# Attention transposes released by the exponentials, and a rotation split over four units

## The chip, the cores and the metric

The kernel runs on one core of one Trainium2 chip. Its five engines take their instructions in order and meet through semaphores: TensorE (PE in the profile; PEld is its weight load) multiplies and transposes into PSUM banks, VectorE (DVE) and ScalarE (ACT) do arithmetic on PSUM and SBUF, GpSimd (POOL) and SyncE (SP) mostly start DMAs. The metric is the device time of one execution in microseconds.

## The reference, cut to what matters

The whole program is a two-layer mixer block, then a gated delta-net block, a sliding-window attention and an eight-expert feed-forward. The change touches three attentions. In each of the two layers there are a differential attention (A), the forgetting attention (B, the "second" one) and a retention (C); the window attention is the "local" one.

```
def _forgetting_attention(q, k, v, log_f):      # B, 4 heads of 128, 256 tokens
    F = jnp.cumsum(log_f, axis=1)
    s = einsum(q, k) * scale + F_q - F_k
    p = softmax(where(causal, s, -inf))
    return p @ v

def _rotary(t, pos):                            # on q and k of the retention C
    t1, t2 = t[..., :half], t[..., half:]
    return concat([t1 * cos - t2 * sin, t1 * sin + t2 * cos])

def swa_sink_attention(...):                    # W, 16 heads of 64, window 128, a sink logit
    p = softmax(concat([s + bias, sink]))[..., :-1]
    return (p @ v) @ w_out
```

B and W keep the softmax's numerator as it comes from the exponential and divide the head's output by the row sum. So what is transposed is the exponential itself, and the reciprocal of the row sum enters only when the output leaves PSUM. A is different: there two maps are scaled by their reciprocals and combined before the transpose.

## The kernel before, in words

Every fp32 weight chunk of 1 MB (a half chunk, 128 x 2048) goes through a fixed path: a DMA into one of four slots `W`, ScalarE's `high(1)` (line 1670, two instructions) rounds it into one of two slots `W_high`, VectorE's `low(1)` (line 2167, two instructions) writes the remainder to `W_low`, and TensorE multiplies it in three products (lines 844 to 846), 24 matmuls for a half chunk. `high` of half chunk n waits until TensorE has done half chunk n-2. This projection work is called the background (`next(bg)`).

The order of every engine is written out by hand. The second attention of a layer is a loop over eight units u = 8 to 15 (four heads, two query tiles; an even u has one key tile, 128 scores a row, an odd u two, 256). In unit u each engine does:

- TensorE: the scores of unit u+1, one half chunk of the background, `attend_T` (line 1056: the transposes of unit u's exponentials, line 1064), `attend_out` of unit u-1 (line 1077). After the last unit come the output of unit 15, the transposes of the rotated q and k ("cT", which wait for `zC_ready`), of A's normed output ("yA", which wait for `y_ready`), and then the next half chunk of the background. That one needs two PSUM banks, of which the second is free only when VectorE has read out the output of unit 15.
- ScalarE: `exps(u+1)` (line 1778), `evict_probsT` of unit u (line 1655, the transposed exponentials to SBUF), `high(1)`; after the `high` of unit 12 also `root(8)` (line 1792), a square root for A's norm, for which the activation table is switched there and back.
- VectorE: `mask_b(u+1)` (lines 2503 and 2505: scores from PSUM plus mask, and the row maximum), the reciprocal of unit u's row sum (line 2764, which signals `probs`), in odd units the bias addition of a finished background chunk (line 2157, two), `b_out(u-1)` (line 2636), `low(1)`, and then extra work: in units 9 and 10 `rotate(t)`, twelve operations for one token tile (lines 2745 to 2755), in unit 12 `sums_a` (sums of squares of A's output), in unit 13 `scale_a` (its norm, which signals `y_ready`). After unit 15 follows `b_out(15)`.

So VectorE's reciprocal of unit u stands behind mask u+1, which stands behind all extra work of unit u-1, and TensorE's `attend_T` of unit u waits for that reciprocal through `probs`. The exponential of unit u, signalled by `exped`, is made one unit earlier.

The window attention has 16 units of the same form with three score buffers; there `window_T(u-1)` comes behind the scores of unit u+1, and VectorE's reciprocal is line 3294. Its projections are woven between the units.

## Time and profile before

| | |
|---|---|
| three runs | 2946.49, 2950.98, 2953.47 us; median 2950.98 |
| the profiled execution | 2955.86 us, of which the span is 2954.0 |
| PE / DVE / ACT busy | 2668.4 / 2180.4 / 1516.2 us (90 / 74 / 51% of the span) |
| mean granted TensorE clock | 0.944 of 2.4 GHz |
| the chain that ended last | PE 63%, DVE 22%, ACT 7%, issue 4%, DMA 3% |
| DMA share by fortieths of the span | 1 to 5 tenths in most of the two layers, 9 in the experts |
| second attention and what follows it, layer 0 | transposes of unit 9 at 238.9 us, next half chunk after the attention at 302.6 |
| the same in layer 1 | 880.3 us and 942.8 |
| window attention | 1808 to 1876 us |

The span is cut by stage, and each stage has its own limit: an average such as TensorE's 90% does not tell whether a given wait of 3 us costs 3 us. A timeline row gives the start, the duration, the engine and the line, and in brackets how long the engine had been idle before and which instruction released it.

### The profile page before, as it was taken

The numbers are of one execution on the slowest core, as the hardware profiler recorded it, in microseconds if no ns is written. First come the engines' busy times: TensorE is split into PE (matmuls) and PEld (weight loads), VectorE is DVE, ScalarE is ACT, GpSimd is POOL, SyncE is SP. The second block draws the span as 40 slices with busy tenths as digits, with TensorE's granted clock in tenths as the row PEclk, the third lists the DMA queues.
The fourth block names the chain that finished last, engine by engine and source line by source line (L and its number), as shares of the span: only waits on it lengthen the run. The fifth ranks groups of instructions, "written<-read, shape, count | busy, mean of one in ns | idle before, by whom it ended". The sixth has DMA issues, their size and how long they took to land.

```text
span 2954.0 us, 36711 instructions
## 1 busy us (share of the span) xinstructions
PE 2668.4 (90%) x14052; PEld 2275.1 (77%) x14052; DVE 2180.4 (74%) x2746; ACT 1516.2 (51%) x1782; POOL 24.2 (1%) x46
## 2 busy tenths in 40 slices
PE   7988888898987889987889987789999999999997
PEld 6766678876776679877788966678888888888885
DVE  6766487778666677755577546678989889898886
ACT  2233434434334345435324334457777777777774
POOL 0000000000000000000000000000000000000000
PEclk9889999999899899988999998789999999999998
DMA  9633345576533355442105582369999998999984
GB/s 357 254 129 131 120 157 213 199 284 247 203 132 128 111 189 207 158 157 101 68 16 183 184 242 100 125 248 368 346 351 367 346 369 344 351 365 347 373 341 184
DMA packets 104753, 671.67 MB, mean 227 GB/s; under 512 B 11984, under 2 KB 12240, under 8 KB 27136
## 3 DMA queue, kind: packets, MB, share of 16 engines
q1 hardware_dynamic: 97584, 622.08, 56.8%
q0 software_dynamic: 6992, 47.19, 4.8%
q8 instruction: 116, 1.90, 0.3%
q14 instruction: 61, 0.50, 0.0%
HBM read 665.03 MB, written 4.19 MB: 227 GB/s over the span
## 4 chain that ended last, share of the span: by engine, by line
PE 63%; DVE 22%; ACT 7%; issue 4%; DMA 3%; PEld 2%; DVEq 0%; SPq 0%; ACTq 0%; PEldq 0%
PE bank L844 18%; PE bank L845 18%; PE bank L846 18%; DVE W_low L2167 8%; ACT W_high L1670 3%; PE bank L1252 3%; DVE work L2252 1%; PE bank L1550 1%; DMA arena<-in_w_layer 1%; DMA W<-in_w_layer 1%; DVE arena L2157 1%; DMA W<-in_w_middle 1%; DVE work L2484 1%; PEld bank L844 1%; DMA R<-in_rows_middle 1%
## 5 line engine op out<-in xcount | busy, mean ns | idle before, releaser
L2167 DVE TENSOR_TENSOR W_low<-W,W_high 128x1024 fp32r<-128x1024 f32 x426 | 496.7, 1207 | 352.6 <-ACT W_high L1670 348.8
L1670 ACT ACTIVATE W_high<-W 128x1024 fp32r<-128x1024 f32 x426 | 422.3, 1040 | 456.0 <-PE bank L846 211.8
L845 PE MATMUL bank<-W_low,arena_parts 128*128 128x512 f32 x1112 | 438.5, 394 | 0.0
L844 PE MATMUL bank<-W_high,arena_parts 128*128 128x512 f32 x968 | 390.8, 404 | 16.0 <-DVE W_low L2167 10.9
L846 PE MATMUL bank<-W_high,arena_parts 128*128 128x512 f32 x968 | 382.7, 395 | 0.0
L846 PE MATMUL bank<-hT_high,W_low 128*128 128x256 f32 x1184 | 340.6, 288 | 0.0
L844 PE MATMUL bank<-hT_high,W_high 128*128 128x256 f32 x1072 | 311.4, 291 | 20.1 <-DVE W_low L2167 12.0
L844 PE MATMUL bank<-W_high,hT_high 128*128 128x512 f32 (+3 forms) x688 | 285.8, 415 | 29.5 <-DVE W_low L2167 10.1
L845 PE MATMUL bank<-hT_low,W_high 128*128 128x256 f32 x1072 | 306.6, 286 | 0.0
L845 PE MATMUL bank<-W_low,hT_high 128*128 128x512 f32 (+4 forms) x736 | 294.0, 399 | 0.0
L846 PE MATMUL bank<-W_high,hT_low 128*128 128x512 f32 (+3 forms) x688 | 274.6, 399 | 0.0
L844 PE MATMUL bank<-arena_parts 128*128 128x512 f32 x672 | 269.3, 401 | 1.5 <-issue 1.5
L846 PE MATMUL bank<-arena_parts 128*128 128x512 f32 x672 | 263.2, 392 | 0.0
L845 PEld LDWEIGHTS bank<-W_low,arena_parts 128*128 128x128 f32 x1112 | 212.3, 191 | 42.9
L846 PEld LDWEIGHTS bank<-hT_high,W_low 128*128 128x128 f32 x1184 | 233.6, 197 | 0.0
L844 PEld LDWEIGHTS bank<-W_high,arena_parts 128*128 128x128 f32 x968 | 185.0, 191 | 60.1 <-DVE W_low L2167 15.0
L844 PEld LDWEIGHTS bank<-hT_high,W_high 128*128 128x128 f32 x1072 | 208.8, 195 | 27.2 <-DVE W_low L2167 17.5
L846 PEld LDWEIGHTS bank<-W_high,arena_parts 128*128 128x128 f32 x968 | 184.5, 191 | 41.0
L845 PEld LDWEIGHTS bank<-hT_low,W_high 128*128 128x128 f32 x1072 | 209.1, 195 | 0.1
L844 PEld LDWEIGHTS bank<-W_high,hT_high 128*128 128x128 f32 x688 | 145.1, 211 | 63.5 <-DVE W_low L2167 22.5
L845 PE MATMUL bank<-arena_parts 128*128 128x512 f32 x456 | 178.2, 391 | 0.0
L845 PEld LDWEIGHTS bank<-W_low,hT_high 128*128 128x128 f32 x736 | 157.1, 213 | 25.5
(418 smaller groups left out, 4884.8 us busy)
## 6 DMA issues: line engine op xcount, KB each, us to landing
W<-in_w_layer SPq DMA_DIRECT2D x170, 1024.0 KB, 4.9
W<-in_w_expert SPq DMA_DIRECT2D x148, 1024.0 KB, 4.8
arena<-in_w_expert SPq DMA_DIRECT2D x114, 1024.0 KB, 5.0
W<-in_w_middle SPq DMA_DIRECT2D x58, 1024.0 KB, 5.0
arena<-in_w_layer POOLq DMA_DIRECT2D x40, 1024.0 KB, 6.4
consts<-in_w_expert SPq DMA_DIRECT2D x37, 1024.0 KB, 4.9
R<-in_w_expert SPq DMA_DIRECT2D x37, 1024.0 KB, 5.0
R<-in_rows_layer SPq DMA_DIRECT2D x70, 256.0 KB, 5.7
```

Of the source, the lines that this page charges most:

```text
L844: mm(bank, lhs[0], rhs[0], start=start, stop=False)
L845: mm(bank, lhs[0], rhs[1], start=False, stop=False)
L846: return mm(bank, lhs[1], rhs[0], start=False, stop=stop)
L1252: last = mm(bank[:, i * P:(i + 1) * P], lhs(i), rhs(i), start=True, stop=True)
L1550: last = turn_over(bank[:, i * P:(i + 1) * P], hid_tok[:, c % 2, i * P:(i + 1) * P], ident)
L1670: do(high_slot(at, w)[:, cols], raw(at, w)[:, cols], ACT.Copy).then_inc(main_highs.filled[main_highs.slot(at, w)], 1)
L2157: tt(dst, bank[:, 0:width], r[:, 0:width], ALU.add).then_inc(*psum.frees(v.at, job))
L2167: tt(lows(at, w)[:, cols], raw(at, w)[:, cols], high_slot(at, w)[:, cols].bitcast(F32), ALU.subtract).then_inc(*low_ready.event(at))
L2252: i = stt(acc, part, csil[:, f:f + 1], acc, ALU.mult, ALU.add)
L2484: stt(c[:, 2:S], u[:, 0:S - 2], taps[:, j:j + 1], c[:, 2:S], ALU.mult, ALU.add).then_inc(*hid_pre.event(v.at))
```

## The change

Two things change. The transposes of the second and of the window attention (not of A) wait for the exponential's signal `exped`, and the rotation is cut in halves: `rotate(t, s)` does six operations, and units 9, 10, 11 and 12 have one half each where units 9 and 10 had two. `zC_ready` is signalled behind units 10 and 12. To make room, `sums_a` moves from unit 12 to 13, `scale_a` from 13 to 14, and ScalarE's `root(8)` from behind unit 12's `high` to behind unit 13's. The number of instructions stays the same on every engine.

```diff
--- before.py
+++ after.py
@@ -1055,7 +1055,7 @@
 
             def attend_T(kind, h_, t, u, maps, src=None):
                 hand_back()
-                pe.wait_ge(*probs.nth(at, u + 1))
+                pe.wait_ge(*(probs if kind == "A" else exped).nth(at, u + 1))
                 pe.wait_ge(*psum.vacant(at, (kind + "t", h_, t)))
                 bank = banks[psum.slot(at, (kind + "t", h_, t))]
                 for m in range(maps):
@@ -1882,7 +1882,7 @@
                         exps(u + 1, (u + 1) % NT, 1)
                     evict_probsT("B", (u - 8) // NT, u % NT, u, 1)
                     high(1)
-                    if u == 12:
+                    if u == 13:
                         root(8)
                 tiles("cT", 2, cT, qkT_ready)
                 high_tiles("yA", 1, yATs)
@@ -2735,25 +2735,24 @@
 
 
 
-                def rotate(t):
-                    for s in range(2):
-                        z = zCqk[:, t, s * 512:(s + 1) * 512].rearrange("p (h f) -> p h f", h=C_HEADS)
-                        t1, t2 = z[:, :, 0:64], z[:, :, 64:128]
-                        w = [work[:, i * 256:(i + 1) * 256].rearrange("p (h f) -> p h f", h=C_HEADS) for i in range(3)]
-                        cs = cos[:, t, :].unsqueeze(1).to_broadcast([P, C_HEADS, 64])
-                        sn = sin[:, t, :].unsqueeze(1).to_broadcast([P, C_HEADS, 64])
-                        tt(w[0], t1, cs, ALU.mult).then_inc(dve_done, 1)
-                        dve.wait_ge(dve_done, v.count())
...
-                        tt(t2, w[0], w[2], ALU.add).then_inc(dve_done, 1)
-                        dve.wait_ge(dve_done, v.count())
+                def rotate(t, s):
+                    z = zCqk[:, t, s * 512:(s + 1) * 512].rearrange("p (h f) -> p h f", h=C_HEADS)
+                    t1, t2 = z[:, :, 0:64], z[:, :, 64:128]
+                    w = [work[:, i * 256:(i + 1) * 256].rearrange("p (h f) -> p h f", h=C_HEADS) for i in range(3)]
+                    cs = cos[:, t, :].unsqueeze(1).to_broadcast([P, C_HEADS, 64])
+                    sn = sin[:, t, :].unsqueeze(1).to_broadcast([P, C_HEADS, 64])
+                    tt(w[0], t1, cs, ALU.mult).then_inc(dve_done, 1)
+                    dve.wait_ge(dve_done, v.count())
...
+                    tt(t2, w[0], w[2], ALU.add).then_inc(dve_done, 1)
+                    dve.wait_ge(dve_done, v.count())
 
                 mask_b(8)
                 for u in range(8, 16):
@@ -2768,12 +2767,13 @@
                     if u > 8:
                         b_out(u - 1)
                     low(1)
-                    if u == 12:
+                    if u == 13:
                         sums_a()
-                    if u == 13:
+                    if u == 14:
                         scale_a()
-                    if u in (9, 10):
-                        rotate(u - 9)
+                    if 9 <= u < 13:
+                        rotate((u - 9) // 2, (u - 9) % 2)
+                    if u in (10, 12):
                         dve.nop().then_inc(*zC_ready.event(v.at))
                 b_out(15)
                 dve.nop().then_inc(*y_ready.event(v.at))
```

On TensorE no instruction moves; only what the first transpose of a unit waits for. The piece below is from the difference of TensorE's instructions with their waits, at unit 9 of layer 0 (`scores` holds the exponentials, `bank_freed` and `product_done` are PSUM hand-overs).

```order
 L846 MATMUL bank<-W_high,hT_low 128x512
-L1064 MATMUL bank<-consts,scores 128x128 [waits product_done1,bank_freed4,probs]
+L1064 MATMUL bank<-consts,scores 128x128 [waits product_done1,bank_freed4,exped]
 L1064 MATMUL bank<-consts,scores 128x128
 L1077 MATMUL bank<-arena,probsT 128x128 [waits bank_freed5,probsT_ready]
```

The signal named at the end of the wait list is the reciprocal's before and the exponential's now; the product and the bank that it also waits for stay.

On VectorE the rotation moves. First as it was, from the end of unit 9's first half rotation on into unit 10, layer 0 (`W_low` is the background's `low`, `small` the row sums):

```order
L2751 TENSOR_TENSOR arena<-work 128x4x64 [waits dve_done]
L2753 TENSOR_TENSOR work<-arena,consts 128x256 [waits dve_done]
L2755 TENSOR_TENSOR arena<-work 128x4x64 [waits dve_done]
L2503 SCALAR_TENSOR_TENSOR scores<-bank,consts 128x256 [waits dve_done,product_done6]
L2505 TENSOR_REDUCE small<-scores 128x1 [waits bank_freed6]
L2764 RECIPROCAL small<-small 128x1 [waits exped,masked]
L2636 TENSOR_SCALAR arena<-bank,small 128x128 [waits product_done2,probs]
```

These are the last three of twelve rotation operations, and the mask of unit 11 and the reciprocal of unit 10 stand behind all twelve. Then the changed kernel at the same place, from the end of unit 9's `low` on:

```order
L2744 TENSOR_TENSOR work<-arena,consts 128x256
L2746 TENSOR_TENSOR work<-arena,consts 128x256 [waits dve_done]
L2748 TENSOR_TENSOR work<-arena,consts 128x256 [waits dve_done]
L2750 TENSOR_TENSOR arena<-work 128x4x64 [waits dve_done]
L2752 TENSOR_TENSOR work<-arena,consts 128x256 [waits dve_done]
L2754 TENSOR_TENSOR arena<-work 128x4x64 [waits dve_done]
L2503 SCALAR_TENSOR_TENSOR scores<-bank,consts 128x256 [waits product_done6,dve_done]
L2505 TENSOR_REDUCE small<-scores 128x1 [waits bank_freed6]
L2763 RECIPROCAL small<-small 128x1 [waits exped,masked]
```

Six operations stand ahead of the mask now; the other six come behind unit 10's `low`, and the same again in units 11 and 12.

On ScalarE the square root with its two table loads moves back by one unit. The piece is from the difference of ScalarE's instructions, layer 0, units 13 and 14 (`probsT` are the transposed exponentials, `W_high` is the background's `high`):

```order
 L1670 ACTIVATE W_high<-W 128x1024 x2
+L1778 ACTIVATE scores,small<-scores,small 128x128
+L1655 ACTIVATE probsT<-bank 128x256
+L1670 ACTIVATE W_high<-W 128x1024 x2
 L1792 ACT_TABLE_LOAD
 L1792 ACTIVATE small<-small 128x8
 L1778 ACT_TABLE_LOAD
-L1778 ACTIVATE scores,small<-scores,small 128x128
-L1655 ACTIVATE probsT<-bank 128x256
-L1670 ACTIVATE W_high<-W 128x1024 x2
 L1778 ACTIVATE scores,small<-scores,small 128x256
```

The exponentials that stand behind the table loads are now those of unit 15, not of unit 14.

## Rows read from the trace of the kernel before

**Rows 1.** What TensorE's transposes (line 1064) waited for: releaser, us in total, times.
```profile
  DVE small L2764: 20.5, 8
  DVE small L3294: 8.3, 5
```
**Rows 2.** Timeline of TensorE, layer 0: transposes of units 9, 10, 11, 13, 14; next half chunk.
```profile
238.94 0.41 PE L1064 MATMUL bank<-consts,scores 128*128 128x128 f32 x2 [0.30 <-PE bank L846]
...
250.49 0.33 PE L1064 MATMUL bank<-consts,scores 128*128 128x128 f32 x1 [3.27 <-DVE small L2764]
...
261.29 0.44 PE L1064 MATMUL bank<-consts,scores 128*128 128x128 f32 x2 [3.88 <-DVE small L2764]
...
279.30 0.44 PE L1064 MATMUL bank<-consts,scores 128*128 128x128 f32 x2 [1.34 <-DVE small L2764]
...
289.46 0.44 PE L1064 MATMUL bank<-consts,scores 128*128 128x128 f32 x1 [1.89 <-DVE small L2764]
...
302.57 0.47 PE L844 MATMUL bank<-W_high,hT_high 128*128 128x512 f32 x1 [0.65 <-DVE arena L2636]
```
**Rows 3.** Timeline of VectorE, layer 0, from unit 9's rotation to unit 10's.
```profile
243.73 0.42 DVE L2745 TENSOR_TENSOR work<-arena,consts 128x256 f32<-128x256 f32 x1
...
248.79 0.42 DVE L2755 TENSOR_TENSOR arena<-work 128x256 f32<-128x256 f32 x1
249.36 0.42 DVE L2503 SCALAR_TENSOR_TENSOR scores<-bank,consts 128x256 f32<-128x256 f32 x1
...
252.53 2.36 DVE L2167 TENSOR_TENSOR W_low<-W,W_high 128x1024 fp32r<-128x1024 f32 x2 [0.79 <-ACT W_high L1670]
254.81 0.42 DVE L2745 TENSOR_TENSOR work<-arena,consts 128x256 f32<-128x256 f32 x1
```
**Rows 4.** Timeline of ScalarE in the same unit: exponentials of unit 11, then `high`.
```profile
250.27 0.51 ACT L1778 ACTIVATE scores<-scores,small 128x256 f32<-128x256 f32 x1 [7.98 <-DVE small L2505]
...
251.37 2.01 ACT L1670 ACTIVATE W_high<-W 128x1024 fp32r<-128x1024 f32 x2 [0.17 <-ACT probsT L1655]
```
**Rows 5.** Timeline of VectorE, layer 0: sums, mask 14, bias additions, norm, mask 15, last output.
```profile
275.34 0.69 DVE L2716 TENSOR_TENSOR work<-arena 128x512 f32<-128x512 f32 x1
...
278.43 0.29 DVE L2503 SCALAR_TENSOR_TENSOR scores<-bank,consts 128x128 f32<-128x128 f32 x1
...
279.28 1.42 DVE L2157 TENSOR_TENSOR h<-bank,R 128x512 f32<-128x512 f32 x2
...
284.95 0.20 DVE L2336 RECIPROCAL small<-small 128x8 f32<-128x8 f32 x1
...
288.33 0.43 DVE L2503 SCALAR_TENSOR_TENSOR scores<-bank,consts 128x256 f32<-128x256 f32 x1 [0.15 <-DVE arena L2732]
...
302.08 0.34 DVE L2636 TENSOR_SCALAR arena<-bank,small 128x128 f32<-128x128 f32 x1
```
**Rows 6.** Timeline of ScalarE: the table load back to the exponential, layer 0.
```profile
279.12 1.28 ACT L1778 ACT_TABLE_LOAD   x1 [0.48 <-DVE small L2505]
```
**Rows 7.** Stretches: us, busy of PE, PEld, DVE, ACT, POOL, granted clock, DMA share, GB/s.
```profile
261.30:265.30 4.00, 4.00 (x15) 3.32 (x15) 3.47 (x5) 2.66 (x5) 0.00 (x0) 0.62 0.25 98
302.60:316.20 13.60, 13.30 (x58) 10.53 (x58) 4.37 (x6) 9.59 (x9) 0.00 (x0) 1.00 0.27 87
```
**Rows 8.** A stretch of layer 1, behind the transposes of unit 11; same columns.
```profile
902.30:907.00 4.70, 4.69 (x13) 3.94 (x14) 3.92 (x5) 2.67 (x5) 0.00 (x0) 0.50 0.23 91
```
**Rows 9.** Timeline of layer 1: VectorE's rotation in unit 9, TensorE's half chunk after the attention.
```profile
884.76 0.42 DVE L2745 TENSOR_TENSOR work<-arena,consts 128x256 f32<-128x256 f32 x1
...
942.78 0.47 PE L844 MATMUL bank<-W_high,hT_high 128*128 128x512 f32 x1 [0.66 <-DVE arena L2636]
```
**Rows 10.** Timeline of the window attention: last step of exponential 0, transposes 0 and 4.
```profile
1808.65 0.19 ACT L2050 ACTIVATION_READ_ACCUMULATOR arena<-arena,small 128x1 f32 x1
...
1810.01 0.69 PE L1064 MATMUL bank<-consts,arena 128*128 128x128 f32 x2 [5.16 <-DVE small L3294]
...
1825.57 0.44 PE L1064 MATMUL bank<-consts,arena 128*128 128x128 f32 x2 [0.77 <-DVE small L3294]
```

More of the change, by code:

```diff
@@ L2734, in scale_a @@
                     dve.nop().then_inc(*rows.frees(v.at, ("gdiff", 0)))
-                def rotate(t):
-                    for s in range(2):
-                        z = zCqk[:, t, s * 512:(s + 1) * 512].rearrange("p (h f) -> p h f", h=C_HEADS)
-                        t1, t2 = z[:, :, 0:64], z[:, :, 64:128]
-                        w = [work[:, i * 256:(i + 1) * 256].rearrange("p (h f) -> p h f", h=C_HEADS) for i in range(3)]
-                        cs = cos[:, t, :].unsqueeze(1).to_broadcast([P, C_HEADS, 64])
-                        sn = sin[:, t, :].unsqueeze(1).to_broadcast([P, C_HEADS, 64])
-                        tt(w[0], t1, cs, ALU.mult).then_inc(dve_done, 1)
-                        dve.wait_ge(dve_done, v.count())
-                        tt(w[1], t2, sn, ALU.mult).then_inc(dve_done, 1)
-                        dve.wait_ge(dve_done, v.count())
-                        tt(w[2], t1, sn, ALU.mult).then_inc(dve_done, 1)
-                        dve.wait_ge(dve_done, v.count())
-                        tt(t1, w[0], w[1], ALU.subtract).then_inc(dve_done, 1)
-                        dve.wait_ge(dve_done, v.count())
-                        tt(w[0], t2, cs, ALU.mult).then_inc(dve_done, 1)
-                        dve.wait_ge(dve_done, v.count())
-                        tt(t2, w[0], w[2], ALU.add).then_inc(dve_done, 1)
-                        dve.wait_ge(dve_done, v.count())
@@ new lines, in rotate @@
+                def rotate(t, s):
[6 more added lines that the diff above has]
+                    dve.wait_ge(dve_done, v.count())
+                    tt(w[1], t2, sn, ALU.mult).then_inc(dve_done, 1)
+                    dve.wait_ge(dve_done, v.count())
+                    tt(w[2], t1, sn, ALU.mult).then_inc(dve_done, 1)
+                    dve.wait_ge(dve_done, v.count())
+                    tt(t1, w[0], w[1], ALU.subtract).then_inc(dve_done, 1)
+                    dve.wait_ge(dve_done, v.count())
+                    tt(w[0], t2, cs, ALU.mult).then_inc(dve_done, 1)
+                    dve.wait_ge(dve_done, v.count())
+                    tt(t2, w[0], w[2], ALU.add).then_inc(dve_done, 1)
+                    dve.wait_ge(dve_done, v.count())
```

## The prediction

> **What bounds the kernel now.** I read the page first: TensorE is busy 90% of the span, so a change pays where it removes TensorE's idle time, and only as far as the next wait lets it. Then I asked what the transposes of line 1064 wait for. The reciprocal of the second attention costs TensorE 20.5 us in 8 waits, that of the window attention 8.3 us in 5 [rows 1]. The timeline of TensorE shows the four waits of layer 0: 3.27, 3.88, 1.34 and 1.89 us, in units 10, 11, 13 and 14, together 10.4; the other 10.1 are layer 1's [rows 2]. The timeline of VectorE shows why. Unit 9's rotation runs from 243.73 to 249.21, twelve operations 0.46 apart, and only behind it come mask 11 (249.36) and the reciprocal that TensorE wants [rows 3]. ScalarE waited 7.98 us for that mask as well, and its `high` of the background follows only at 251.37 [rows 4]; VectorE's `low` waits for that `high` (252.53), and the next rotation for `low` (254.81) [rows 3]. So there is a closed loop of VectorE and ScalarE: rotation, mask, exponential, `high`, `low`, 254.81 - 243.73 = 11.1 us a unit. TensorE alone needs less. Its transposes of unit 10 could have gone at 250.49 - 3.27 = 247.2, 8.3 after unit 9's, and unit 11's at 261.29 - 3.88 = 257.4, 6.9 after unit 10's [rows 2]. So TensorE's own pace is 8.3 us up to an even unit and 6.9 to 7.2 up to an odd one.
>
> **The waits that go.** The exponential of unit u is made in unit u-1, ahead of the extra work, so with `exped` all four waits of a layer go; nothing else that TensorE asks for there is later than before. If that were all, a layer would gain 10.4. But VectorE and ScalarE keep their loop, and the attention ends for TensorE when VectorE has read out unit 15: the half chunk at 302.57 waited for line 2636, whose row starts at 302.08 [rows 2, 5]. So I work out when VectorE comes there.
>
> **The loop with a half rotation.** Six operations of 0.46 leave: 11.08 - 2.76 = 8.32 us for a unit whose mask is of two key tiles. With one tile the mask's first operation is 0.13 shorter (0.29 against 0.42 [rows 3, 5]); I take the maximum to be so too, and the shorter exponential to make up for the longer copy of the transposes beside it: 8.05. Unit 9's `low` ends at 243.73 as before (nothing ahead of it changes). The next ends: 252.05 (unit 10), 260.10 (11), 268.42 (12), 276.47 (13). Half rotations stand in all four, so the loop is 8.2 a unit where TensorE needs 7.6 in the mean. TensorE has one unit of slack, because a half chunk is made ready one unit ahead of its use, and does not wait.
>
> **The tail.** Behind unit 13's `low` stands `sums_a` now. Before, 275.34 (its start) to 284.95 (the norm's first operation) was 9.61 us [rows 5], with mask 14, the root, the table load (1.28 [rows 6]) and ScalarE's copy and `high` in it. The same sequence now has mask 15 in it, 0.27 longer: 276.47 + 9.88 = 286.35. The norm took 288.33 - 284.95 = 3.38 [rows 5]: 289.73. Then come the reciprocal (0.2), two bias additions (1.42 [rows 5], 1.45 with the gap), the output of unit 14 (0.4), the last `low` (2.28, 254.81 - 252.53 [rows 3]; its `high` is long done, since ScalarE no longer waits for anything of VectorE's) and the output of unit 15 with the hand-over (0.34 + 0.15): 294.6. TensorE gets there earlier: its units 10 to 15 at 247.2, 254.4, 262.7, 269.8, 278.1 and 284.7, then the last outputs and the 24 transposes of "cT" and "yA". "yA" waits some 0.5 us for the norm; TensorE is done at 290.1 and stands 4.5 us, where it stood 0.65.
>
> So layer 0 gains 302.57 - 294.6 = 8.0 us, not 10.4 plus what follows from it. Layer 1 took 942.78 - 884.76 = 58.0 us for the same stretch [rows 9] where layer 0 took 302.57 - 243.73 = 58.8. With 294.6 - 243.73 = 50.9 it gains 7.1. Together 15.1.
>
> **The window attention.** There is no rotation; the wait is for the mask of the next unit. Exponential 0 ended at 1808.84, the transposes went at 1810.01 [rows 10]: with 0.1 for the hand-over 1.1 us come back. Unit 4's 0.77 [rows 10] come back too. The other three waits (8.3 - 5.16 - 0.77 = 2.4 us together [rows 1, 10]) I count as nothing: VectorE's own chain (mask, maximum, reciprocal, output, late query) sets there when the bank of the following output is free. Bounds: 0 and 1.1 + 0.77 + 2.4 = 4.3; I take 1.9.
>
> **The clock.** In layer 0 TensorE stood 3.9 us ahead of unit 11's transposes [rows 2], and in the next 4.0 us its granted clock was 0.62 in the mean, that is, mostly 1.2 GHz instead of 2.4: 1.5 us lost [rows 7]. In layer 1 it was 0.50 over 4.7 us at the same place: 2.35 lost [rows 8]. These drops leave with the idle time, but that is already in the loop's sum, which TensorE's own pace does not set. What is new is the 4.5 us stand ahead of the half chunk. By the rows of 3.9 us it costs a drop, and there TensorE is what ScalarE's next `high` waits for: mean 1.9 us a layer, 3.8 in all, bounds 0 and 2 x 2.35. "TensorE: Matmul & The Clock Gate" of the Trainium skill, the section on practical rules for kernels, says that an idle gap between bursts of matmuls puts the array back to half rate. By that rule every such stand is charged and the sum is the one below; without it it would be 3.8 us faster. The trace agrees only in part: the 3.27 us ahead of unit 10 were followed by no drop.
>
> **Sum.** 15.1 + 1.9 - 3.8 = 13.2 us. The profiled execution took 2955.86, the change gives 2942.7. That execution was 4.9 above the median of the runs, 2950.98; from the median it is 2937.8, and I say 2938. The moved square root, sums and norm are counted in the tail. Nothing is added on SP or POOL, and the projections, the experts and their transfers start relative to what TensorE frees, so they move along.
>
> **Rivals.**
> - *No new clock drop*, everything else as above: gain 17.0, 2934. For it: the stand of 3.27 us without a drop, and the norm's transposes shortly ahead of the stand. Against: both stands of 3.9 us (layer 0 [rows 2] and its like in layer 1 [rows 8]) had one. 0.20.
> - *All waits pay*: 20.5 us of the layers, 3.9 for the two clock drops, 4.3 in the window: 28.7, 2922. It needs VectorE to come to unit 15's output 5 us earlier than in my chain. Against it is the loop of rows 3 and 4. 0.08.
> - *The gain is taken up behind the attention*, or the two edits do the same thing twice and less than the chain says: TensorE arrives at the retention earlier, but what it waits for there (the stretch 302.60 to 316.20 has ScalarE busy 9.6 of 13.6 us [rows 7]) hangs on ScalarE and VectorE, which stay where they were. Then about 6 us a layer are taken back and 3 us are left: 2948. Against: ScalarE's next `high` there needs this very half chunk to be done. 0.14.
> - *Slower*: the new stand ahead of the half chunk lets the clock fall, and in the retention, where the work is thin, it does not come back for long. The stretch from 302.60 to 316.20 ran at 1.00 [rows 7]; at 1.2 GHz throughout it would take 13.6 us more in each layer, 27.2, less the 17.0 gained: 10.2 slower, 2961. It decides from a drop of 17 us on (8.5 us lost in each layer). The longest that I have a row of is 4.7 us [rows 8]. 0.06.
>
> **How the numbers follow.** My forecast has 0.52; its own range is 2934 to 2942 (window 0 to 4.3, clock 0 to 4.7, a microsecond in each tail). The range for 8 in 10 leaves out the lower half of "all waits pay", most of "taken up" and "slower": 2927 to 2947. Runs of this kernel tell a change from none at about 0.2%, 5.9 us. Faster by more: 0.52 + 0.20 + 0.08 + 0.02 = 0.82; within: 0.12; slower: 0.06.
>
> **What would show it.** No transposes of line 1064 wait for line 2764's successor in the second attention, and unit 11's go near 254.4. VectorE's `low` ends stand 8.0 to 8.4 us apart in units 10 to 13. The half chunk after the attention starts near 294.6 in layer 0 with a wait of 4 to 5 us on VectorE's last output, followed by a low clock. I am wrong if transposes still wait there for something (the exponential or a bank), if the half chunk starts later than 297, or if it starts on time and the retention is longer by more than 3 us.

## The result and the profile after

| | before | after |
|---|---|---|
| median of 6 runs | 2953.34 us (2946.49 to 2954.12) | 2937.80 us (2932.71 to 2943.08) |
| ratio of the two | 1 | 0.995, 95% interval 0.9935 to 0.9965 |
| profiled execution (its span) | 2955.86 (2954.0) | 2943.08 (2941.2) |
| layer 0: unit 9's transposes to the half chunk after the attention | 63.63 | 55.59 |
| layer 1: the same | 62.52 | 55.15 |
| from that half chunk to the retention's first output (line 1181), layers 0 / 1 | 12.11 / 12.13 | 13.05 / 12.53 |
| window attention, first scores to the first projection transposes behind it (line 901) | 73.76 | 74.32 |

The kernel is 0.5% faster: 15.5 us at the medians, 12.8 in the two profiled executions. The profile's 12.8 is the sum of its stages: 8.04 and 7.37 gained up to the half chunk, 0.94 and 0.40 lost behind it, 0.56 lost in the window, and 0.7 lost on balance elsewhere, where nothing was changed. The profiled execution of the kernel after is the slowest of its six. Everything in layer 0 stands 0.74 us later in this execution than in that of before (unit 9's transposes at 239.68, [rows 2]: 238.94); compare after taking that off.

What TensorE's transposes (line 1064) waited for, in the kernel after (releaser, us, times); it answers to [rows 1]:

```profile
  DVE scores L2690: 16.9, 11
  ACT arena L2050: 4.0, 1
  PE bank L846: 2.8, 9
  DVE arena_parts L2215: 2.4, 1
```

The two reciprocals, 20.5 and 8.3 us before, are gone. In their place stands one wait of 4.0 us, for the window's first exponential. Where a reciprocal was waited for, a transpose now waits at most 0.3 us for TensorE's own last product: that is the third row, 1.5 us in 5 waits before. The other two have nothing to do with the edit (the first is of the differential attention).

TensorE's timeline, layer 0 after, against [rows 2]: transposes of units 9, 10 and 11, unit 14's half chunk, transposes of units 14 and 15, then the end of the stage.

```profile
239.68 0.41 PE L1064 MATMUL bank<-consts,scores 128*128 128x128 f32 x2 [0.30 <-PE bank L846]
...
247.81 0.27 PE L1064 MATMUL bank<-consts,scores 128*128 128x128 f32 x1
...
254.97 0.41 PE L1064 MATMUL bank<-consts,scores 128*128 128x128 f32 x2 [0.30 <-PE bank L846]
...
274.14 0.47 PE L844 MATMUL bank<-W_high,hT_high 128*128 128x512 f32 x1 [0.70 <-DVE h L2157]
...
279.67 0.27 PE L1064 MATMUL bank<-consts,scores 128*128 128x128 f32 x1
...
286.14 0.41 PE L1064 MATMUL bank<-consts,scores 128*128 128x128 f32 x2 [0.30 <-PE bank L846]
...
287.64 0.60 PE L901 MATMUL bank<-consts,arena 128*128 128x128 f32 x4
291.09 4.53 PE L901 MATMUL bank<-consts,arena 128*128 128x128 f32 x20 [2.85 <-DVE arena L2157]
295.27 0.78 PE L844 MATMUL bank<-W_high,hT_high 128*128 128x512 f32 x1
```

The four waits of the loop are gone, and unit 11's transposes go at 254.97 where they went at 261.29. Two new waits are there, and neither names an exponential or a reciprocal. Both name line 2157, the bias addition that reads a finished background chunk out of PSUM and gives its two banks back: 0.70 us ahead of unit 14's half chunk, and 2.85 after the first four of the 24 transposes. The half chunk itself waits for nothing. In layer 1 the same stand was 2.81 us, and there the half chunk still waited 0.15 us for VectorE's last output:

```profile
923.84 3.82 PE L901 MATMUL bank<-consts,arena 128*128 128x128 f32 x20 [2.81 <-DVE arena L2157]
927.81 0.77 PE L844 MATMUL bank<-W_high,hT_high 128*128 128x512 f32 x1 [0.15 <-DVE arena L2636]
```

VectorE's timeline, layer 0 after, against [rows 3] and [rows 5]: the first operation of each of the four half rotations, of the sums and of the norm, and the tail.

```profile
244.47 0.42 DVE L2744 TENSOR_TENSOR work<-arena,consts 128x256 f32<-128x256 f32 x1
...
252.66 0.42 DVE L2744 TENSOR_TENSOR work<-arena,consts 128x256 f32<-128x256 f32 x1
...
260.68 0.42 DVE L2744 TENSOR_TENSOR work<-arena,consts 128x256 f32<-128x256 f32 x1
...
268.87 0.42 DVE L2744 TENSOR_TENSOR work<-arena,consts 128x256 f32<-128x256 f32 x1
...
276.91 0.69 DVE L2716 TENSOR_TENSOR work<-arena 128x512 f32<-128x512 f32 x1
...
286.78 0.20 DVE L2336 RECIPROCAL small<-small 128x8 f32<-128x8 f32 x1
...
290.15 0.16 DVE L2763 RECIPROCAL small<-small 128x1 f32<-128x1 f32 x1
290.35 1.42 DVE L2157 TENSOR_TENSOR arena<-bank,R 128x512 f32<-128x512 f32 x2
291.91 0.35 DVE L2636 TENSOR_SCALAR arena<-bank,small 128x128 f32<-128x128 f32 x1
292.30 2.36 DVE L2167 TENSOR_TENSOR W_low<-W,W_high 128x1024 fp32r<-128x1024 f32 x2
294.57 0.34 DVE L2636 TENSOR_SCALAR arena<-bank,small 128x128 f32<-128x128 f32 x1
```

The rotations start 8.19, 8.02 and 8.19 us apart, where the loop of before had 11.08. Behind the norm stand the two bias additions of 290.35. TensorE had finished their chunk 4.5 us before (at 285.84); its transposes at 291.09 want one of the banks that they read.

Stretches of the kernel after (us, busy time of each engine, granted clock, DMA share, GB/s), against [rows 7]:

```profile
261.30:265.30 4.00, 4.00 (x25) 3.47 (x24) 3.32 (x9) 0.88 (x3) 0.00 (x0) 1.00 0.18 29
289.00:294.20 5.20, 3.11 (x15) 3.10 (x16) 4.77 (x8) 2.08 (x5) 0.00 (x0) 0.63 0.36 134
294.20:299.00 4.80, 4.80 (x19) 4.07 (x18) 0.72 (x2) 1.55 (x3) 0.00 (x0) 0.69 0.00 0
299.00:304.00 5.00, 5.00 (x25) 4.17 (x23) 0.93 (x1) 2.01 (x2) 0.00 (x0) 1.00 0.18 41
```

The old drop behind unit 11 is gone (0.62 before, 1.00 now). A new one follows the 2.85 us stand and lasts into the half chunk; by 299 the clock is back.

### The profile page after: what moved, and what is told of

Same layout as the page of the kernel before. It is cut to its first block, busy times and chain, and to the rows that moved or that the text cites. A ratio compares the mean times of both kernels' runs of the same rounds, so it can differ in the third digit from the quotient of the medians.

```text
span 2941.2 us, 36715 instructions
## 1 busy us (share of the span) xinstructions
PE 2668.3 (91%) x14052; PEld 2277.3 (77%) x14052; DVE 2179.6 (74%) x2746; ACT 1514.9 (52%) x1782; POOL 24.2 (1%) x46
## 4 chain that ended last, share of the span: by engine, by line
PE 62%; DVE 22%; ACT 7%; issue 4%; DMA 3%; PEld 2%; DVEq 0%; SPq 0%; ACTq 0%; PEldq 0%
PE bank L844 18%; PE bank L846 18%; PE bank L845 18%; DVE W_low L2167 8%; ACT W_high L1670 3%; PE bank L1252 3%; DVE work L2252 1%; PE bank L1550 1%; DMA W<-in_w_layer 1%; DVE arena L2157 1%; DMA W<-in_w_middle 1%; DVE work L2484 1%; PEld bank L844 1%; PEld bank L846 1%; PEld bank L845 1%
## 5 line engine op out<-in xcount | busy, mean ns | idle before, releaser
L844 PEld LDWEIGHTS bank<-W_high,arena_parts 128*128 128x128 f32 x968 | 184.8, 191 | 60.6 <-DVE W_low L2167 15.4
```

What stands on the lines that cost most here:

```text
L844: mm(bank, lhs[0], rhs[0], start=start, stop=False)
```

## The experiments

The experiments ran in three groups (e1 to e4, e5 to e8, e9 and e10), each with its own runs of the kernel before beside it: medians 2951.49, 2952.03 and 2952.55 us, and 2953.34 beside the kernel after. So ratios are compared rather than times, and where the intervals overlap the text does not claim a difference in time. "Half chunk" is the time from unit 9's transposes to the half chunk after the attention, layers 0 / 1; "window" is the stage as in the table above. Both are from each kernel's profile.

| kernel | median us | ratio [95%] | half chunk | window |
|---|---|---|---|---|
| before | 2951.5 to 2952.6 | 1 | 63.63 / 62.52 | 73.76 |
| after | 2937.80 | 0.995 [0.9935, 0.9965] | 55.59 / 55.15 | 74.32 |
| e1 wait edit alone | 2943.85 | 0.9976 [0.9967, 0.9985] | 59.13 / 58.90 | 71.56 |
| e2 rotation edit alone | 2942.16 | 0.9968 [0.9956, 0.9981] | 57.92 / 56.66 | 74.60 |
| e3 window on the reciprocal | 2934.68 | 0.995 [0.9936, 0.9965] | 55.59 / 55.14 | 74.09 |
| e4 work moved ahead | 2923.78 | 0.9915 [0.9899, 0.9932] | 49.82 / 49.59 | 74.37 |
| e5 whole rotations, units 9 and 11 | 2933.35 | 0.9934 [0.9916, 0.9952] | 55.38 / 55.07 | 71.64 |
| e6 last output first | 2934.33 | 0.9943 [0.9925, 0.996] | 54.81 / 55.46 | 70.98 |
| e7 rotation ahead only | 2928.47 | 0.9916 [0.9898, 0.9934] | 53.59 / 53.68 | 71.46 |
| e8 sums not moved | 2935.08 | 0.9938 [0.992, 0.9955] | 57.42 / 55.10 | 71.39 |
| e9 as e4, on the reciprocal | 2936.66 | 0.9942 [0.9928, 0.9956] | 53.81 / 53.48 | 73.77 |
| e10 window edit alone | 2947.22 | 0.9987 [0.9975, 0.9998] | 63.59 / 61.65 | 71.50 |

**e1: before, with the wait edit alone.** The rotation stays whole, in units 9 and 10. Of the two theories in the text below, theory 1 is that of the forecast: VectorE's and ScalarE's loop and its tail set the end.

```diff
-                pe.wait_ge(*probs.nth(at, u + 1))
+                pe.wait_ge(*(probs if kind == "A" else exped).nth(at, u + 1))
```

> The kernel before with only the wait changed: the transposes of the second and the window attention wait for the exponentials, the rotation stays in units 9 and 10. Theory 1 (the VectorE/ScalarE loop and its tail set the end of the attention, so the two edits are two ways to the same saving): the loop still does all its work once, so the half chunk after the attention starts 54.8 us after unit 9's transposes (63.6 before, 55.6 with both edits), VectorE's extra work only stands elsewhere; 2938, within 2 us of the kernel with both edits. Rival (TensorE's own waits are what was paid, and each edit removes its share): the rotation's share stays, the half chunk starts after about 59, and half of the 15.5 us is missing, 2945.

59.13 and 2943.85: the rival's numbers came out. TensorE's timeline of this kernel, unit 12's half chunk and the half chunk after the attention:

```profile
262.14 0.76 PE L844 MATMUL bank<-W_high,hT_high 128*128 128x512 f32 x1 [5.78 <-DVE h L2157]
...
297.40 0.47 PE L844 MATMUL bank<-W_high,hT_high 128*128 128x512 f32 x1 [1.28 <-DVE arena L2636]
```

And VectorE's, the end of unit 10's rotation and what stands behind it:

```profile
259.16 0.42 DVE L2755 TENSOR_TENSOR arena<-work 128x256 f32<-128x256 f32 x1
259.73 0.29 DVE L2503 SCALAR_TENSOR_TENSOR scores<-bank,consts 128x128 f32<-128x128 f32 x1
...
260.57 1.42 DVE L2157 TENSOR_TENSOR h<-bank,R 128x512 f32<-128x512 f32 x2
```

The waits of the transposes became one wait of 5.78 us (5.50 in layer 1) a little later. A chunk holds two banks until its bias additions, and these stand behind unit 10's whole rotation and mask 12. The reciprocal was only the first of VectorE's results that TensorE needs from behind the rotation; the bank is the second. VectorE gives it back no later than before (the additions start 22.3 us after unit 9's transposes in both kernels); TensorE comes for it sooner. What theory 1 missed is that VectorE's chain is not closed either: in unit 12 VectorE itself stands 4.68 us for an output of TensorE (at 270.64), so TensorE's wait for the banks comes back to it. The rival is right only in part as well, since the half chunk still waits 1.28 us for VectorE's last output.

**e2: after, with the wait edit taken back.** All transposes wait for `probs` again; the half rotations and the later sums stay.

```diff
-                pe.wait_ge(*(probs if kind == "A" else exped).nth(at, u + 1))
+                pe.wait_ge(*probs.nth(at, u + 1))
```

> The changed kernel with its first edit undone: every transpose waits for the reciprocals again, the rotation is spread over four units and the sums, norm and root stand one unit later. Theory 1: small waits of 0.1 to 0.8 us in units 10 to 14 and one of 2.4 us ahead of unit 15 (its mask stands behind the sums and its exponential behind the table load), the half chunk after the attention 55.3 us after unit 9's transposes; 14 us below the kernel before, nothing from the window attention: 2939 to 2940. Rival (the savings add up): what the first edit does not give, 2945 or more.

57.92 / 56.66 and 2942.16: in between the two. What the transposes waited for in this kernel, and its longest wait, ahead of unit 15 in layer 0:

```profile
  DVE small L2763: 11.8, 9
  DVE small L3294: 8.3, 5
```
```profile
287.55 0.69 PE L1064 MATMUL bank<-consts,scores 128*128 128x128 f32 x2 [2.96 <-DVE small L2763]
```

The rotation edit alone brings the second attention's wait for the reciprocal from 20.5 us to 11.8. Theory 1 had 2.4 us ahead of unit 15; it was 2.96, and the granted clock of the next 4 us was 0.50 in layer 0 and 0.67 in layer 1. e1 gained 7.6 us at the medians and e2 9.3, 16.9 together; both edits in one kernel gained 15.5. With the width of the intervals (2.7 to 4.4 us to either side) that does not show whether they add up. The stage does: up to the half chunk e1 gained 4.50 / 3.62 and e2 5.71 / 5.86, which is 10.2 / 9.5 together, and both edits gained 8.04 / 7.37. So some 2 us a layer are in both.

**e3: after, with the window back on the reciprocal.**

```diff
-                pe.wait_ge(*(probs if kind == "A" else exped).nth(at, u + 1))
+                pe.wait_ge(*(exped if kind == "B" else probs).nth(at, u + 1))
```

> The changed kernel, with the window attention's transposes waiting for the reciprocals again. By the forecast's term for the window attention 1.9 us slower than the changed kernel, 2939.7. By the two profiles (73.8 us for that stage before, 74.3 changed) the term is nothing, because what is saved at units 0 and 4 goes to a clock drop behind unit 5: 2938, within 1 us, and the stage takes 73.8 us again with the waits of 5.2, 0.8, 1.0, 1.0 and 0.4 us back.

The same ratio as the kernel after, and a stage as long. Intervals of some 4 us to either side would hide the 1.9 us of the forecast, so the time does not settle what the window edit is worth here; the stage shows nothing gained in the two profiled executions. e10 below shows a gain.

**e5: after, with whole rotations, far enough apart.** e1 showed bias additions (in odd units) caught behind unit 10's rotation. Here each rotation is whole, but stands at the end of an odd unit, so that the next mask only is behind it and the next bias additions are a unit away.

```diff
-                    if 9 <= u < 13:
-                        rotate((u - 9) // 2, (u - 9) % 2)
-                    if u in (10, 12):
+                    if u in (9, 11):
+                        rotate((u - 9) // 2, 0)
+                        rotate((u - 9) // 2, 1)
                         dve.nop().then_inc(*zC_ready.event(v.at))
```

> The changed kernel with the rotation whole again, in units 9 and 11 (both tiles' operations as before, twelve each), everything else as changed. It asks why the waits' edit alone gave only half: there half chunk 12 stood 5.8 us for PSUM banks that VectorE's bias additions of unit 11 give back, behind unit 10's whole rotation. Bank theory: here no whole rotation stands between unit 10's low and those additions, so half chunk 12 waits under 1 us; the second rotation delays the sums and with them the additions of unit 13 by at most 1.5 us. The half chunk after the attention starts 56 to 57 us after unit 9's transposes (55.6 changed, 59.1 with the waits' edit alone): 2938 to 2940. Rival (the split itself is needed, since a whole rotation holds mask and exponential wherever it stands): 59, 2944.

As fast as the kernel after (55.38 / 55.07), with its waits (0.71 and 2.81). The half chunk came 0.6 and 0.9 us sooner than bank theory had it, and the median, 2933.35, is 5 us under its 2938. So it is not the split that is needed. With the exponential's signal, spacing is enough: e1 has a whole rotation directly ahead of a unit with bias additions and e5 has none. The two differ in the place of sums, root and norm as well, so the 3.8 us between their half chunks are not all the rotation's; e1's wait of 5.78 us is.

**e6: after, with unit 15's output ahead of the last `low`.** The prediction had TensorE stand ahead of the half chunk for this very output.

```diff
                         b_out(u - 1)
+                    if u == 15:
+                        b_out(15)
                     low(1)
...
-                b_out(15)
                 dve.nop().then_inc(*y_ready.event(v.at))
```

> The changed kernel, only with VectorE's output of unit 15 ahead of its last low instead of behind it (2.3 us sooner). The forecast's own picture (TensorE stands 4.5 us ahead of the half chunk for that output) says 2.3 us a layer, 2933. The trace of the changed kernel says that TensorE stood 2.9 us earlier, for the bank that the bias additions of unit 15 hold, and had the transposes still to do when the output was read: no difference, 2938 within 1.5, the half chunk again 55 to 55.6 us after unit 9's transposes.

54.81 / 55.46 where it was 55.59 / 55.15: no difference, and the bank wait is still 2.81 and 2.85. The forecast's place for the wait falls. The test has one weakness. The half chunk followed the bank by 3.42 and 3.98 us (granted clock 0.68 and 0.61 in the 4 us behind the stand), where in e9, at full clock, it began 2.54 us after the first of all 24 transposes. So in e6 TensorE's slow transposes, and no longer VectorE's output, set the end, and where the clock stays up the early output could be worth up to 1 or 2 us a layer (an estimate from these rows, which no run tests).

**e8: after, with root, sums and norm back in units 12, 12 and 13.**

```diff
                     high(1)
-                    if u == 13:
+                    if u == 12:
                         root(8)
...
-                    if u == 13:
+                    if u == 12:
                         sums_a()
-                    if u == 14:
+                    if u == 13:
                         scale_a()
```

> The changed kernel with sums, root and norm back in units 12, 12 and 13 (where the kernel before has them), beside unit 12's half rotation. Chain theory: the tail behind the last exponential gets shorter by about 1 us a layer, but the sums now stand ahead of unit 13's bias additions, so half chunk 14 waits 3.8 us for their banks (0.7 in the changed kernel) and TensorE comes later to the end: the half chunk after the attention 55.5 to 56.5 us, 2938 to 2940. Rival (the norm is what ends the attention): 53.5, 2934.

TensorE's timeline of this kernel, layer 0, unit 14's half chunk and the one after the attention:

```profile
275.52 0.76 PE L844 MATMUL bank<-W_high,hT_high 128*128 128x512 f32 x1 [3.80 <-DVE h L2157]
...
295.40 0.47 PE L844 MATMUL bank<-W_high,hT_high 128*128 128x512 f32 x1 [0.66 <-DVE arena L2636]
```

Sums and half rotation stack up ahead of unit 13's bias additions, and unit 14's half chunk waits 3.80 us (3.79 in layer 1), as expected. The end hardly moves in layer 1 (55.10), because the norm is then out of the tail; layer 0 (57.42) had a clock drop behind the stand (granted 0.50 in the next 4 us), layer 1 had none (1.00). Neither half chunk is where chain theory (55.5 to 56.5) or the rival (53.5) had it. The median, 2935.08, is nearer the rival's 2934, but the time cannot be told from the kernel after's. The trace decides: what the end gains by an earlier norm goes into the new wait.

**e7: after, with the rotation moved ahead.** Unit 8 has little to do on VectorE; tile 0 is rotated there, ahead of `low`, and tile 1's halves in units 9 and 10.

```diff
+                    if u == 8:
+                        rotate(0, 0)
+                        rotate(0, 1)
+                        dve.nop().then_inc(*zC_ready.event(v.at))
                     low(1)
...
-                    if 9 <= u < 13:
-                        rotate((u - 9) // 2, (u - 9) % 2)
-                    if u in (10, 12):
+                    if u in (9, 10):
+                        rotate(1, u - 9)
+                    if u == 10:
                         dve.nop().then_inc(*zC_ready.event(v.at))
```

> The changed kernel with only the rotation placed anew: both halves of the first token tile in unit 8 ahead of its low, those of the second in units 9 and 10; sums, norm and root stay in units 13, 14 and 13. It splits the gain of the run with everything moved ahead (13.9 us below the changed kernel, 49.8 us instead of 55.6). VectorE's chain theory: units 11 and 12 have no extra work, so VectorE waits for TensorE there and comes to the sums 2 us sooner; the tail (sums, norm, additions, low) is as long as before: the half chunk after 53 to 53.5 us, the bank wait 0.5 to 1 us, 2932 to 2934. Rival (only the last units count): no difference, 2938.

53.59 / 53.68, as expected up to 0.2 us. The bank wait is 1.96 us, twice what was expected, and the median 3.5 us under the forecast. The end of the stage, layer 0:

```profile
286.94 2.69 PE L901 MATMUL bank<-consts,arena 128*128 128x128 f32 x20 [1.96 <-DVE arena L2157]
290.91 0.47 PE L844 MATMUL bank<-W_high,hT_high 128*128 128x512 f32 x1 [1.28 <-DVE arena L2636]
```

VectorE comes sooner to the tail because it has no extra work in units 11 and 12. Here the clock stayed up, and the half chunk does wait for VectorE's last output.

**e4: e7, with sums, root and norm one unit earlier and unit 15's output ahead of the last `low`.** The edit is that of e7 and, on top of it, with `root(8)` moved as in e8:

```diff
+                    if u == 15:
+                        b_out(15)
                     low(1)
-                    if u == 13:
+                    if u == 12:
                         sums_a()
-                    if u == 14:
+                    if u == 13:
                         scale_a()
...
-                b_out(15)
```

> The changed kernel with VectorE's work put where it stood idle: both half rotations of the first token tile in unit 8, ahead of its low (5.2 us idle there in both profiles), those of the second in units 9 and 10, sums, root and norm in units 12, 12 and 13 as in the kernel before, and the output of unit 15 read ahead of the last low. Theory 1 (VectorE's chain sets the end of the attention and 5.5 us of it now lies in idle time): the half chunk after it starts 49.9 us after unit 9's transposes, TensorE's own pace, 5 us sooner than in the changed kernel, without the 2.9 us wait for a bank; 9 to 10 us below the changed kernel, 2928 to 2930. Rival (TensorE is the limit once its waits for the reciprocals are gone): no difference, 2938.

49.82 / 49.59, as worked out. TensorE's timeline at the end of the stage, layer 0:

```profile
282.90 3.00 PE L901 MATMUL bank<-consts,arena 128*128 128x128 f32 x24
285.65 0.47 PE L844 MATMUL bank<-W_high,hT_high 128*128 128x512 f32 x1
```

All 24 transposes in one piece of 3.00 us and the half chunk at once behind them. No wait of 0.45 us or more is left between unit 9 and the retention, in either layer, and the clock stays at full. This version beats both kernels: 27.7 us less than before beside it at the medians (0.85% by the ratio), where the kernel after had 15.5 (0.5%). The time is 4 us under the forecast. The stage accounts for 5.77 and 5.56 us over the kernel after. By the ratio e4 (0.9915) cannot be told from e7 (0.9916), though its half chunks come 3.8 and 4.1 us sooner.

**e9: e4, with the transposes waiting for the reciprocal again.** Is the wait edit still needed once the work is out of the way?

```diff
-                pe.wait_ge(*(probs if kind == "A" else exped).nth(at, u + 1))
+                pe.wait_ge(*probs.nth(at, u + 1))
```

> The kernel with the work moved ahead, but all transposes wait for the reciprocal again. In that kernel's profile (layer 0) the reciprocals end at 244.45, 252.46, 257.9, 267.75 and 277.91 for units 10 to 14, and the transposes went at 243.95, 251.12, 259.6, 266.8 and 274.9. Theory 1 (the wait still costs where masks stand behind sums and norm): stands of about 0.5, 1.4, 0, 1.0 and 3.0 us, which overlap more than they add; half chunk 53 to 54 us after unit 9's transposes where it was 49.8, time 2929 to 2932. Rival (once the rotation is out of the way the wait for the exponential is needless): half chunk at 50 to 50.5, 2923 to 2925.

TensorE's timeline of this kernel, units 11, 13 and 14 of layer 0:

```profile
253.98 0.44 PE L1064 MATMUL bank<-consts,scores 128*128 128x128 f32 x2 [1.12 <-DVE small L2763]
...
270.34 0.44 PE L1064 MATMUL bank<-consts,scores 128*128 128x128 f32 x2 [1.33 <-DVE small L2763]
...
280.50 0.33 PE L1064 MATMUL bank<-consts,scores 128*128 128x128 f32 x1 [1.85 <-DVE small L2763]
```

It is: 53.81 / 53.48, 4 us a layer, and theory 1 had the stage right. The profiled executions differ by 8.4 us (spans 2930.3 and 2921.9), of which the two layers are 7.9. By the ratios (0.9942 and 0.9915) they differ by 8 us as well. The median of e9, 2936.66, is 5 to 8 us above the forecast; its profiled execution, 2932.21, is the fastest of its six, and stands just above it.

**e10: before, with the wait edit in the window only.**

```diff
-                pe.wait_ge(*probs.nth(at, u + 1))
+                pe.wait_ge(*(exped if kind == "W" else probs).nth(at, u + 1))
```

> The kernel before with one edit: the window attention's transposes alone wait for the exponential; the second attention is as it was (half chunk 63.6 and 62.5 us after unit 9's transposes). Theory 1 (the window stage has two courses, with and without a drop of the clock, and the edit gains where there is none): the stage takes 71 to 71.7 us where it took 73.8, time 2 to 3 us less, 2948 to 2950 beside 2951.5 of the kernel before. Rival (nothing is gained in the window, the drop that comes with it takes it back): stage 73.5 to 74.5, time within 1 us of the kernel before.

71.50 where it was 73.76, and 0.9987 with an interval that just excludes 1: theory 1. In layer 1 the half chunk came 0.9 us sooner (61.65) though nothing was changed there: one clock drop fell away and another came (last section). The same stretch in this kernel, from unit 5's output on (it waits 1.47 us there for a bias addition), and in the kernel after, where it waits 1.46:

```profile
1821.92:1831.92 10.00, 8.56 (x56) 7.67 (x56) 4.85 (x19) 4.29 (x13) 0.00 (x0) 0.83 0.30 110
```
```profile
1819.52:1829.52 10.00, 9.50 (x50) 8.58 (x50) 3.63 (x15) 2.72 (x9) 0.00 (x0) 0.66 0.16 41
```

The instructions and the wait are the same; the granted clock is not. Over the whole stage TensorE's 368 matmuls were busy for 61.62 us in the kernel after and for 58.87 in e10, and these 2.75 us are nearly all of the 2.82 between the two stages. Of the eight profiles with the exponential's signal in the window, six took 71.0 to 71.6 us and two (after and e4) 74.3 and 74.4; the four with the reciprocal took 73.8 to 74.6.

## Why the prediction was right, and where its picture was not

The forecast was 2938.0 from a median of 2950.98; measured were 2937.8, with the kernel before at 2953.34 beside it. That the two agree to 0.2 us is luck: the gain at the medians was 15.5 where 13.2 were forecast, and the kernel before stood 2.4 us higher than in the three runs that the forecast started from. Against the profile's own gain of 12.8 stands the forecast sum of 13.2. There the part on the two layers is right for its reasons (15.4 us where 15.1 were forecast), and the agreement of the rest is luck again: the window gave 2.5 us less than forecast, and the clock took 2.5 us less than forecast. By its steps:

- *The loop with a half rotation*: held. Taking off the 0.74 us, the `low` ends of units 10 to 13 were forecast at 252.05, 260.10, 268.42 and 276.47 and came at 251.92, 259.94, 268.13 and 276.17.
- *The tail*: held. The norm was to start at 286.35 and did at 286.04; the half chunk was to go at 294.6 and went at 294.53. So 8.0 and 7.1 became 8.04 and 7.37. That VectorE's chain sets the end and the removed 20.5 us do not come back whole is shown by e7 and e4 as well: taking work off VectorE's tail moves the half chunk by 2.0 / 1.5 and by 5.8 / 5.6 us, with no wait of line 1064 left to remove. In layer 0 it was close: TensorE's own slow transposes ended 0.2 us after VectorE's output would have let the half chunk go.
- *TensorE's own pace*: units 10 to 13 within 0.2 us; units 14 and 15 came 0.8 and 0.7 late. "Nothing else that TensorE asks for there is later than before" does not carry what was drawn from it. The banks come back no later than before, but TensorE comes for them sooner: it waited 0.70 us for one ahead of unit 14's half chunk. It cost nothing, since TensorE stands afterwards anyway.
- *The place of the stand*: wrong, and one of the prediction's own signs, a wait of 4 to 5 us ahead of the half chunk, did not appear (none in layer 0, 0.15 us in layer 1). I had 0.5 us for the norm and 4.5 ahead of the half chunk. TensorE stood 2.85 us in the middle of the transposes, for the bank of unit 15's background chunk, which I had as two bias additions in VectorE's sum and never as something that TensorE waits for. e6 tests my place: the half chunk moves by 0.8 us one way in layer 0 and by 0.3 the other way in layer 1, where 2.3 sooner were asked for.
- *The clock*: the drop came, at 1.3 us in the place of 3.8 (0.94 + 0.40 behind the half chunk). The 20 transposes took 4.53 us at a granted clock of 0.50 where e7's took 2.69 at full clock; these 1.8 us lie beside VectorE's last `low` and output, which end at 294.91, and the half chunk could not have gone much before 295.06. Had the stand been where I put it, the drop would have begun with the half chunk, with nothing to hide it; so I read the wrong size as following from the wrong place, though no run shows that by itself.
- *The window*: forecast 1.9, in the kernel after's profile -0.6. The wait of 5.16 became 4.04 as forecast (1.1), and the later waits turned into waits for the output's bank, as forecast. e10 shows 2.3 where the clock stays up. So the term was about right for six of the eight profiled executions with this edit (2.1 to 2.8 us less than before's 73.76), and the profiled one of after is among the other two.
- *The range*: its lower end, 2934, does not follow from its own terms. Window 4.3, clock 0 and a microsecond in each tail give 2930; 2934 is the time of the rival without a clock drop.

What I had not seen, and the result does not show, is what e1 shows. All four waits of a layer do go with `exped`, as the prediction says, but with the rotation in its old place 5.8 us come back at once as one wait for the banks. I had worked out the two edits together only, and so the forecast came out right without knowing this. The trace of the kernel before could have told it. Unit 11's bias additions stand behind unit 10's rotation there too, 22.3 us after unit 9's transposes; in e1 TensorE, freed of its wait, asks for their banks at 18.1:

```profile
261.27 1.42 DVE L2157 TENSOR_TENSOR h<-bank,R 128x512 f32<-128x512 f32 x2
```

The rivals: "no new clock drop" (2934) asked for a clock that stays up, and it fell behind the stand in both layers (0.50 and 0.67 in the next 4 us); its time lies at the edge of the measured interval (0.9935 is 2934), so the time alone would not rule it out. "All waits pay" (2922) fell to VectorE's chain; it takes e4's other order to get there. "Taken up behind the attention" asked for 6 us a layer lost in the retention; 0.9 and 0.4 were. The slower case asked for a clock drop of 17 us; the one that came was over by 299, some 8 us after it was first seen.

Left open: what decides between the window's two courses, and how often a stand is followed by a clock drop.

## What to carry to other kernels

When a wait is moved to an earlier signal, list everything else that the waiting engine needs from behind the same work: here the reciprocal was followed at once by the PSUM banks that only a bias addition gives back, and the edit alone gave 8.1 us in the two layers' stages where its waits there held 20.5. What ends a stage is then the tail of the engine that has the extra work, so moving that work into units with slack (e4: 5.8 and 5.6 us more a layer for the same work) was worth more here than cutting it in equal pieces. Work out two edits apart as well as together, since one may only pay beside the other.

## What the runs showed of the hardware

How long TensorE stood did not decide by itself whether its clock fell. Stretches of 4 us (1.00 is 2.4 GHz, 0.50 is 1.2) behind stands in this stage: after 1.96 us (e7) 1.00; after 2.25 (e10, layer 1) 1.00; after 2.81 (e5) 0.61; after 2.85 (after) 0.50; after 2.96 (e2) 0.50; after 3.26 (e10, layer 0, unit 10) 1.00; after 3.80 and 3.79 (e8, layers 0 and 1) 0.50 and 1.00; after 3.86 (e10, unit 11) 0.62; after 5.78 (e1) 0.50. The clearest pair is one place of two kernels that have the same code there, unit 10 of layer 1, where the kernel before stood 2.98 us and e10 2.97:

```profile
891.50:895.50 4.00, 3.99 (x23) 3.52 (x24) 2.30 (x3) 2.69 (x5) 0.00 (x0) 1.00 0.33 137
```
```profile
881.38:885.38 4.00, 4.00 (x16) 3.67 (x17) 2.31 (x3) 2.67 (x5) 0.00 (x0) 0.57 0.30 123
```

The first is the kernel before, the second e10. At the next stand the two changed places: before stood 3.86 us and dropped to 0.50, e10 stood 2.25 and stayed at 1.00. "TensorE: Matmul & The Clock Gate" of the Trainium skill, the section on why this matters for your kernels, goes by the length of an idle gap between bursts of matmuls in saying when the array falls back to half rate. The trace does not agree for gaps as short as these: 2.81 to 2.96 us had a drop in three kernels, 3.26 and 3.79 had none. Yet it is not plain chance either: all ten stands of 2.79 to 2.96 us at the end of the stage (in after, e2, e3, e5 and e6) had one, with 0.50 to 0.68 behind them. What else decides is not shown. So a term for the clock is a chance times a price, and the price depends on what the slow stretch lies beside: 1.8 us of it cost nothing under VectorE's tail, while in e8 the half chunk of layer 0, with a drop, came 2.3 us later than that of layer 1, without one (57.42 against 55.10; the two layers of the kernel after differ by 0.4).
